# Hybrid retention and sparse-attention layer: norm weights applied before the transposes, rounding read straight from PSUM, a score accumulator zeroed in advance

## The chip, the core and the metric

One NeuronCore of a Trainium2 chip runs the whole layer as one program. The metric is the device time of one execution in microseconds, lower is better. Engines go by the profile's names: PE (TensorE matmul), PEld (its weight load), DVE (VectorE), ACT (ScalarE), POOL (GpSimd), SP (SyncE, which here only issues DMAs).

## What is computed

```
z = rmsnorm(x, norm_g) @ w_in            # x: 512 prompt tokens and 8 sample tokens, 2048 wide
q_r,k_r,v_r,g_r, q_a,k_a,v_a,g_a, q_i,k_i,w_i = split(z)
# group A: retention with rotary phase on q_r,k_r,v_r
# group B: indexer  score = sum_h w_i[h] * relu(q_i[h] . k_i);  keep the best keys per query;
#          softmax attention over those keys (samples also over 4096 cached keys each)
x = x + concat(A, B) @ w_out ;  y = rmsnorm(x, final_norm_g)
```

Every product with a weight matrix is done in three matmuls on values split in two: `Hh` is the activation rounded to the fp32r type, `Hl` the rest, and `Wh`, `Wl` the same of the weights; the sum is Wh·Hh + Wh·Hl + Wl·Hh. The first columns that are computed are the index keys `k_i` (128 columns) and the index weights `w_i` (16 columns), since the selection of keys needs them first. They are called chunk 0; their split weights are the tiles `W0h` (which also holds the high and the low part of the 16 columns side by side) and `W0l`.

## The kernel before

Each engine has its own instruction list, written out by hand; the order within a list is the order in the source, and engines meet at semaphores only.

The opening stage makes `Hh` and `Hl`. The 520 tokens are five tiles that arrive in the order 0, 1, 4, 2, 3 (tile 4 is the 8 samples; `ARRIVAL`). For every tile ACT sums the squares (`squares`), DVE makes the reciprocal root in a chain of 12 tiny operations (`norms`, first for tiles 0 and 1, then for the other three together) and multiplies the tile by it (`scale`). PE turns the tile, 2048 columns in 16 transposes, four to a PSUM bank, in banks 4 to 7 in rotation (`turn_tokens`, L1469). DVE multiplies each bank by the norm weights and writes it to SBUF (`gains`, L1017, into the idle tile `mix`), ACT rounds that to `Hh` (`high`, L577), and POOL subtracts the two to make `Hl` (L850), except for the last tile, where DVE does it (L1051). A bank may be filled again once `gains` has read it.

Meanwhile ACT rounds the chunk 0 weights (`hi`, L479) and DVE makes their low parts (`first_weights_low`, L1028 and L1030). PE then multiplies: index keys for tokens 0 to 255 (`index_keys(a, 0)` for the two halves a of the contraction), index weights, index keys for tokens 256 to 519 (`index_keys(a, 1)`), index weights again, and goes on with chunk 1 (`chunk(1, 0)`, L1451 to L1453). From there PE runs through chunks 1 to 8 (the index queries). Their low parts are made by POOL (L836), which takes the chunks in order once it has finished with the tokens.

After chunk 8 comes the scoring of the prompt: 48 rounds (16 heads times 3 blocks of queries) in which PE multiplies, ACT takes the relu and DVE adds it with its weight to the accumulator `bm`. The first head of a block writes `bm` (L1090), the other 15 add to it (L1088):

```
if h:
    v_.scalar_tensor_tensor(r, relu, wn, r, ALU.mult, ALU.add)
else:
    v_.tensor_scalar(r, relu, wn, None, ALU.mult)
```

ACT may not go on to the cached keys before all 48 are added. The rest of the program (cached keys, the selection, the other chunks, the output) is not touched.

Of the kernel before, what the change touches and what calls it, by code (L numbers as in the profile page):

```python
# [37 lines left out]
P = 128  # L38
DM = 2048
# [37 lines left out]
def build(nc, x_prompt, x_sample, cache_k, cache_v, cache_kidx, state_ret, page_table, norm_g, w_in,  # L77
# [3 lines left out]
    with ctx:  # L81
# [12 lines left out]
        mix = sb("mix", [P, KT, NT])  # L94
        ident = sb("ident", [P, P])
# [41 lines left out]
        W0h, _ = place("W0h", [P, KT, P + 2 * NIH], F32R, at["XT"][0])  # L137
        W0l, _ = place("W0l", [P, KT, P], F32R, at["junk"][0])
# [77 lines left out]
        def raw_tile(v, r):  # L216

            v = v % 16
            return mix[:, :, :].rearrange("p k t -> p (k t)")[:, 512 * v:512 * v + 512].rearrange("p (k t) -> p k t", k=4)[:, :, 0:r]

        bank = [ctx.enter_context(nc.psum_tensor(f"bank{i}", [P, 512], F32)) for i in range(8)]

# [3 lines left out]
        x_sq = sem("x_sq"); st4_set = sem("st4_set"); g_tr = sem("g_tr"); x_norm = sem("x_norm"); x_tr = sem("x_tr"); x_g = sem("x_g")  # L226
        h_hi = sem("h_hi"); h_lo = sem("h_lo"); h_lo_last = sem("h_lo_last")
# [107 lines left out]
        def _(sp):  # L335
# [29 lines left out]
            sp.wait_ge(x_in[1], 16)  # L365
# [99 lines left out]
        def _(act):  # L465
# [7 lines left out]
            def hi(n, a, step=None):  # L473
# [106 lines left out]
            for i in ARRIVAL:  # L580
# [250 lines left out]
        def _(pool):  # L831
# [13 lines left out]
            for pos in range(4):  # L845
                i = ARRIVAL[pos]
                for g in range(4):
                    v = 4 * pos + g
                    pool.wait_ge(h_hi, v + 1)
                    nc.gpsimd.tensor_tensor(Hl[:, 4 * g:4 * g + 4, tok(i)], raw_tile(v, rows(i)),  # L850
                                            Hh[:, 4 * g:4 * g + 4, tok(i)].bitcast(F32), ALU.subtract).then_inc(h_lo, 1)
# [114 lines left out]
        def _(dve):  # L966
# [42 lines left out]
            def gains(pos):  # L1009

                r = rows(ARRIVAL[pos])
                for g in range(4):
                    v = 4 * pos + g
                    dve.wait_ge(x_tr, v + 1)
                    if v >= 16:
                        dve.wait_ge(h_lo, v - 15)
                    v_.tensor_tensor(raw_tile(v, r),  # L1017
                                     bank[4 + v % 4][:, :].rearrange("p (k t) -> p k t", k=4)[:, :, 0:r],
                                     gin[:, 4 * g:4 * g + 4].unsqueeze(2).to_broadcast([P, 4, r]), ALU.mult).then_inc(x_g, 1)
# [906 lines left out]
```

## Time and profile before

| | us |
|---|---|
| median of 3 runs | 1240.18 (1239.47 to 1242.28) |
| the profiled execution | 1243.3, of which the span is 1241.5 |
| PE busy over the span | 1170.8 (94%) |
| DVE, ACT, POOL busy | 637.2, 452.3, 577.5 |

The span is the stretch that the trace covers; 1.8 us of the execution lie around it. Three views are used below: the timeline (instructions of one engine in order of time, with the idle time ahead of them), the table by windows (busy time of each engine and the clock granted to PE as a share of 2.4 GHz, in stretches between given times), and the table by groups of instructions. Times in rows count from the start of the span.

### The profile page before, as it was taken

To read this page: it belongs to the slowest core of one execution; us is meant where nothing else is said; L and a number is where in the kernel's file an instruction comes from. 1 tells how busy PE (TensorE), PEld (TensorE's weight loads), DVE (VectorE), ACT (ScalarE), POOL (GpSimd) and SP (SyncE) were. 2 spreads that over 40 slices of the span, in tenths; PEclk is the share of its full clock that TensorE was granted. 3 is DMA by queue.
4 is the path that set the end of the run, shared out by engine and by line. 5 is a ranking of instruction groups with operands and counts; after the bars stand their busy time and mean duration, and the time that the engine had idled before them with its cause. 6 is when DMAs were issued, how large, how long until landed. Compare 5 with 4: busy or idle time off the path is not lost.

```text
span 1241.5 us, 21876 instructions
## 1 busy us (share of the span) xinstructions
PE 1170.8 (94%) x9132; PEld 1109.9 (89%) x9132; DVE 637.2 (51%) x1201; ACT 452.3 (36%) x790; POOL 577.5 (47%) x267
## 2 busy tenths in 40 slices
PE   2899998988999999999999998999999998999995
PEld 2799997544999999999999998999999998999995
DVE  6700003898896997599998405254434537000013
ACT  5322323766223333333424232543434253323332
POOL 3525456042224222332536386848556474445450
PEclk9899998999999999999999999999999999999998
DMA  5423435185142321323343414454453424532313
GB/s 205 136 77 101 135 105 164 69 271 171 35 136 71 101 69 39 101 69 82 84 111 86 128 45 121 130 145 112 129 148 107 120 92 154 173 102 68 101 34 138
DMA packets 152838, 138.57 MB, mean 112 GB/s; under 512 B 4652, under 2 KB 145052, under 8 KB 151068
## 3 DMA queue, kind: packets, MB, share of 16 engines
q1 hardware_dynamic: 144500, 110.71, 29.9%
q0 software_dynamic: 6976, 22.03, 5.5%
q10 hardware_dynamic: 1280, 4.66, 1.0%
q8 instruction: 61, 1.00, 0.3%
q14 instruction: 21, 0.17, 0.0%
HBM read 127.01 MB, written 10.34 MB: 111 GB/s over the span
## 4 chain that ended last, share of the span: by engine, by line
PE 82%; DVE 10%; DMA 4%; issue 2%; ACT 1%; POOL 0%; DVEq 0%; ACTq 0%
PE bank L1451 24%; PE bank L1452 23%; PE bank L1453 23%; PE bank L1469 4%; DMA kx<-in_cache_kidx,pidx 3%; DVE bm L1088 2%; PE bank L1641 1%; PE bank L1659 1%; DVE cand L1154 1%; DVE top L1150 1%; DVE besti L1152 1%; DVE Hl L1051 1%; DMA XT<-in_x_prompt 1%; PE bank L1681 1%; DVE mix L1017 0%
## 5 line engine op out<-in xcount | busy, mean ns | idle before, releaser
L1451 PE MATMUL bank<-Hh,Wh 128*128 128x264 f32 (+2 forms) x2432 | 712.0, 293 | 2.1 <-DVE Hl L1288 0.8
L1452 PE MATMUL bank<-Hl,Wh 128*128 128x264 f32 (+2 forms) x2432 | 703.7, 289 | 0.6 <-issue 0.6
L1453 PE MATMUL bank<-Hh,Wl 128*128 128x264 f32 (+2 forms) x2432 | 702.4, 289 | 1.7 <-issue 1.6
L836 POOL TENSOR_TENSOR Wl<-Wraw,Wh 128x2048 fp32r<-128x2048 f32 x84 | 387.8, 4617 | 472.6 <-ACT Wh L484 472.2
L1451 PEld LDWEIGHTS bank<-Hh,Wh 128*128 128x128 f32 x2432 | 459.7, 189 | 6.7 <-issue 4.2
L1452 PEld LDWEIGHTS bank<-Hl,Wh 128*128 128x128 f32 x2432 | 459.7, 189 | 3.6 <-issue 3.3
L1453 PEld LDWEIGHTS bank<-Hh,Wl 128*128 128x128 f32 x2432 | 458.8, 189 | 2.8 <-issue 2.7
L484 ACT ACTIVATE Wh<-Wraw 128x2048 fp32r<-128x2048 f32 x84 | 160.4, 1911 | 365.9 <-PE bank L1453 365.7
L1391 DVE TENSOR_TENSOR Y<-Y,bank 128x512 f32 (+1 forms) x16 | 10.4, 685 | 159.2 <-PE bank L1469 159.2
L1072 DVE COPY QS<-mix 128x128 f32<-128x128 f32 x1 | 0.3, 281 | 146.1 <-ACT mix L490 146.1
L861 POOL DMA_INDIRECT kx<-in_cache_kidx,pidx x32 | 30.6, 955 | 55.8 <-PE bank L1469 48.8
L1469 PEld LDWEIGHTS bank<-ident,kx 128*128 128x128 f32 x256 | 27.3, 141 | 25.0 <-DMA kx<-in_cache_kidx,pidx 12.3
L1469 PE MATMUL bank<-ident,kx 128*128 128x128 f32 x256 | 34.5, 279 | 8.5 <-DMA kx<-in_cache_kidx,pidx 5.1
L1118 DVE MAX8 best<-scores 32x8 f32<-32x1025 f32 x32 | 38.9, 1217 | 6.7 <-ACT scores L673 5.7
L646 ACT ACTIVATE kT<-bank 128x512 f32<-128x512 f32 x64 | 35.0, 609 | 19.7 <-PE bank L1469 9.9
L891 POOL TENSOR_TENSOR XS<-XS,rot 128x520 f32<-128x520 f32 x16 | 21.1, 1321 | 44.5 <-ACT XW L542 44.5
L1150 DVE MAX8 top<-cand 8x8 f32<-8x1024 f32 x32 | 38.9, 1215 | 1.0
L1549 PE MATMUL bank<-kiT,mix 128*128 128x256 f32 (+2 forms) x96 | 34.6, 524 | 4.6 <-ACT relu L629 3.8
L1120 DVE FIND_INDEX8 besti<-best,scores 32x8 uint32<-32x1025 f32 x32 | 38.6, 1207 | 0.0
L1152 DVE FIND_INDEX8 besti<-top,cand 8x8 uint32<-8x1024 f32 x32 | 38.6, 1205 | 0.0
L1154 DVE MATCH_REPLACE8 cand<-top,cand 8x1024 f32<-8x1024 f32 x32 | 38.3, 1197 | 0.0
L1122 DVE MATCH_REPLACE8 scores<-best,scores 32x1025 f32<-32x1025 f32 x31 | 37.2, 1200 | 0.0
(251 smaller groups left out, 1243.6 us busy)
## 6 DMA issues: line engine op xcount, KB each, us to landing
Wraw<-in_w_in SPq DMA_DIRECT2D x36, 1024.0 KB
Wraw<-in_w_in SPq DMA_DIRECT2D x64, 512.0 KB
Wraw<-in_w_out SPq DMA_DIRECT2D x16, 1024.0 KB
XT<-in_x_prompt ACTq DMA_DIRECT2D x4, 1024.0 KB, 8.7
sp__99<-in_state_ret SPq DMA_DIRECT2D x8, 512.0 KB, 4.2
out<-sp__99 SPq DMA_DIRECT2D x8, 512.0 KB, 5.0
Y<-in_x_prompt SPq DMA_DIRECT2D x1, 4096.0 KB
out<-Y SPq DMA_DIRECT2D x4, 1024.0 KB
```

Source lines behind the costliest of these rows:

```text
L484: nc.scalar.activation(Wh[:, a, :, :], Wraw[:, a, :, :], ACT.Copy).then_inc(w_hi, 1)
L836: nc.gpsimd.tensor_tensor(Wl[:, a, :, :], Wraw[:, a, :, :], Wh[:, a, :, :].bitcast(F32), ALU.subtract).then_inc(w_lo, 1)
L1118: link(v_.max(top, row))
L1120: link(v_.max_index(besti[:, 8 * (k // 3):8 * (k // 3) + 8], top, row))
L1122: link(v_.match_replace(row, top, row, TAKEN))
L1150: link(v_.max(top, cand[:, :]))
L1152: link(v_.max_index(besti[0:NS, 8 * (k // 3):8 * (k // 3) + 8], top, cand[:, :]))
L1154: link(v_.match_replace(cand[:, :], top, cand[:, :], TAKEN))
L1451: mm(bank[i][:, 0:w], wh, Hh[:, kk, s], start=(a == 0 and k == 0), stop=False)
L1452: mm(bank[i][:, 0:w], wh, Hl[:, kk, s], start=False, stop=False)
L1453: last = mm(bank[i][:, 0:w], wl, Hh[:, kk, s], start=False, stop=(a == 1 and k == KC - 1))
L1469: return nc.tensor.transpose(out, in_, ident[0:k, 0:k])
```

## The change

1. The norm weights are no longer multiplied in after the transposes. A new DMA spreads `norm_g` over all partitions into a 128x2048 tile `gb`; it is the third load of ACT's queue. `scale` becomes one scalar_tensor_tensor that multiplies a tile by its reciprocal root and by `gb`. `gains` and the copy in `mix` are gone.
2. ACT rounds to `Hh` straight from the PSUM bank, and DVE makes all of `Hl`, reading the same bank (`low`). A bank may be filled again only when `low` has read it.
3. POOL makes the low parts of the chunk 0 weights in place of DVE. The tiles `W0h` and `W0l` lie in `mix` now, so ACT's rounding of them no longer waits for the transposes.
4. SP starts the weight loads when tile 2 has landed, not tile 1.
5. PE's list is in another order, and the index keys of tokens 256 to 519 are computed as tokens 256 to 383 and then 384 to 519.
6. `bm` is zeroed once (`memset`) when all tokens are done, and all 16 heads of a block use scalar_tensor_tensor.

```diff
@@ SP
-            sp.wait_ge(x_in[1], 16)
+            sp.wait_ge(x_in[2], 16)
@@ ACT, hi
                 if n == 0:
-                    act.wait_ge(x_tr, 8)
@@ ACT, high
-                    act.wait_ge(x_g, v + 1)
-                    nc.scalar.activation(Hh[:, 4 * g:4 * g + 4, tok(i)], raw_tile(v, rows(i)),
+                    act.wait_ge(x_tr, v + 1)
+                    nc.scalar.activation(Hh[:, 4 * g:4 * g + 4, tok(i)], turned_tile(v, rows(i)),
@@ ACT, loads of the tiles
+                if pos == 1:
+                    act.dma_start(gb[:, :], norm_g[0].partition_broadcast(P)).then_inc(g_row, 16)
@@ POOL
-            for pos in range(4):
...
-                    nc.gpsimd.tensor_tensor(Hl[:, 4 * g:4 * g + 4, tok(i)], raw_tile(v, rows(i)),
-                                            Hh[:, 4 * g:4 * g + 4, tok(i)].bitcast(F32), ALU.subtract).then_inc(h_lo, 1)
+            for a in range(2):
+                pool.wait_ge(w_hi, a + 1)
+                k = slice(KC * a, KC * a + KC)
+                nc.gpsimd.tensor_tensor(W0l[:, k, :], Wraw[:, a, :, 0:P], W0h[:, k, 0:P].bitcast(F32), ALU.subtract)
+                nc.gpsimd.tensor_tensor(W0h[:, k, P + NIH:P + 2 * NIH], Wraw[:, a, :, P:P + NIH],
+                                        W0h[:, k, P:P + NIH].bitcast(F32), ALU.subtract).then_inc(w_lo, 1)
+            pool.wait_ge(x_norm, 5)
             lo_loop(1, 10)
@@ DVE
-                v_.tensor_scalar(XT[0:r, i, :], XT[0:r, i, :], st4[0:r, column(i):column(i) + 1], None,
-                                 ALU.mult).then_inc(x_norm, 1)
+                v_.scalar_tensor_tensor(XT[0:r, i, :], XT[0:r, i, :], st4[0:r, column(i):column(i) + 1], gb[0:r, :],
+                                        ALU.mult, ALU.mult).then_inc(x_norm, 1)
+            def low(pos):
+                i = ARRIVAL[pos]
                 for g in range(4):
                     v = 4 * pos + g
+                    dve.wait_ge(h_hi, v + 1)
+                    v_.tensor_tensor(Hl[:, 4 * g:4 * g + 4, tok(i)], turned_tile(v, rows(i)),
+                                     Hh[:, 4 * g:4 * g + 4, tok(i)].bitcast(F32), ALU.subtract).then_inc(h_lo, 1)
...
+            link(v_.memset(bm[:, :], 0.0))
@@ DVE, scoring
-                        v_.scalar_tensor_tensor(r, relu[:, i % 2, 0:w], wn[:, t, h:h + 1], r, ALU.mult, ALU.add).then_inc(si_acc, 1)
-                    else:
-                        v_.tensor_scalar(r, relu[:, i % 2, 0:w], wn[:, t, h:h + 1], None, ALU.mult).then_inc(si_acc, 1)
+                    v_.scalar_tensor_tensor(r, relu[:, i % 2, 0:w], wn[:, t, h:h + 1], r, ALU.mult, ALU.add).then_inc(si_acc, 1)
@@ PE, turn_tokens
-                        pe.wait_ge(x_g, v - 3)
+                        pe.wait_ge(h_lo, v - 3)
@@ PE, chunk 0
-            pe.wait_ge(w_lo, 1)
             pe.wait_ge(h_lo, 8)
-            index_keys(0, 0)
+            pe.wait_ge(w_lo, 1)
+            index_keys(0, slice(0, CUT))
+            pe.wait_ge(w_lo, 2)
+            index_keys(1, slice(0, CUT)).then_inc(acc_done, 1)
             turn_tokens(2)
+            index_weights(slice(P, CUT))
             turn_tokens(3)
             turn_tokens(4)
-            pe.wait_ge(w_lo, 2)
-            index_keys(1, 0).then_inc(acc_done, 1)
-            index_weights(slice(P, CUT))
             pe.wait_ge(h_lo, 16)
-            pe.wait_ge(h_lo_last, 4)
-            index_keys(0, 1)
-            index_keys(1, 1).then_inc(acc_done, 1)
+            for a in range(2):
+                index_keys(a, slice(CUT, CUT + P))
+            pe.wait_ge(h_lo, 20)
+            for a in range(2):
+                last = index_keys(a, slice(CUT + P, NT))
+            last.then_inc(acc_done, 1)
             index_weights(slice(CUT, NT)).then_inc(acc_done, 2)
```

The order of two lists shows the move. DVE, before, from the end of the second `norms` to the page table's product (`XT` is a token tile, `W0l` and `W0h` the chunk 0 weights, `ptm` the page table's product):

```order
L986 SCALAR_TENSOR_TENSOR st<-rsq 128x3 [waits dve_chain]
L1028 TENSOR_TENSOR W0h<-Wraw,W0h 128x8x16 [waits w_hi,dve_chain]
L1030 TENSOR_TENSOR W0l<-Wraw,W0h 128x1024
L1006 TENSOR_SCALAR XT<-XT,st 8x2048
L1006 TENSOR_SCALAR XT<-XT,st 128x2048
...
L1017 TENSOR_TENSOR mix<-bank,gains_T 128x4x8 [waits x_tr] x4
...
L1017 TENSOR_TENSOR mix<-bank,gains_T 128x512 [waits h_lo,x_tr] x4
L1051 TENSOR_TENSOR Hl<-mix,Hh 128x4x128 [waits h_hi] x4
L1059 TENSOR_TENSOR ptm<-ptb,cols 128x256 [waits h_lo,h_lo_last,s_ptab,s_const]
```

The same stretch of DVE after the change:

```order
L989 SCALAR_TENSOR_TENSOR st<-rsq 128x3 [waits dve_chain]
L1018 TENSOR_TENSOR Hl<-bank,Hh 128x4x128 [waits h_hi,dve_chain]
L1018 TENSOR_TENSOR Hl<-bank,Hh 128x4x128 [waits h_hi] x7
L1009 SCALAR_TENSOR_TENSOR XT<-XT,st,gb 8x2048
L1009 SCALAR_TENSOR_TENSOR XT<-XT,st,gb 128x2048 x2
L1018 TENSOR_TENSOR Hl<-bank,Hh 128x4x8 [waits h_hi] x4
L1018 TENSOR_TENSOR Hl<-bank,Hh 128x4x128 [waits h_hi] x8
L1043 MEMSET bm 128x1280 [waits h_lo,s_ptab,s_const]
L1044 TENSOR_TENSOR ptm<-ptb,cols 128x256 [waits dve_chain]
```

The weights' low parts have left this list, the last three `scale` stand behind the `low` of tiles 0 and 1, and every `Hl` is here. PE, before, where the second half of the index keys begins (all rows of this stretch are index keys of 264 tokens; 48 of them):

```order
L1495 MATMUL bank<-Hh,W0h 128x264 [waits h_lo_last,h_lo]
L1496 MATMUL bank<-Hl,W0h 128x264
L1497 MATMUL bank<-Hh,W0l 128x264
```

After the change PE has 48 rows of the first kind below, and then 48 of the second:

```order
L1480 MATMUL bank<-Hh,W0h 128x128 [waits h_lo]
L1481 MATMUL bank<-Hl,W0h 128x128
...
L1480 MATMUL bank<-Hh,W0h 128x136 [waits h_lo]
L1481 MATMUL bank<-Hl,W0h 128x136
```

48 matmuls of 264 columns have become 96 of 128 or 136, each with its own load of 128 columns of weights.

## Rows read from the trace of the kernel before

**Rows 1.** PE by windows: busy, granted clock, DMA share, GB/s.
```profile
25.70:30.40 4.70, 0.00 (x0) 0.50 0.00 0
30.40:35.80 5.40, 5.36 (x24) 0.50 0.68 204
...
51.50:56.20 4.70, 4.70 (x21) 0.50 0.71 223
56.20:63.40 7.20, 7.20 (x61) 0.99 0.48 148
```
**Rows 2.** Timeline of PE: start, duration, line, out<-in, idle before and its releaser.
```profile
45.80 0.22 PE L1504 MATMUL bank<-Hh,W0h 128*32 128x128 f32 x1
45.86 0.22 PE L1505 MATMUL bank<-Hl,W0h 128*32 128x128 f32 x1
...
51.49 0.56 PE L1495 MATMUL bank<-Hh,W0h 128*128 128x264 f32 x1 [5.17 <-DVE Hl L1051]
...
63.45 0.34 PE L1451 MATMUL bank<-Hh,Wh 128*128 128x392 f32 x1
```
**Rows 3.** Timeline of DVE and POOL, 13 to 31 us.
```profile
13.34 2.48 DVE L1006 TENSOR_SCALAR XT<-XT,st 128x2048 f32<-128x2048 f32 x2
...
17.84 9.89 POOL L850 TENSOR_TENSOR Hl<-mix,Hh 128x512 fp32r<-128x512 f32 x8 [17.38 <-ACT Hh L577]
...
18.40 3.22 DVE L1017 TENSOR_TENSOR mix<-bank,gains_T 128x512 f32<-128x512 f32 x5 [0.16 <-PE bank L1469]
...
26.56 1.19 DVE L986 SCALAR_TENSOR_TENSOR rsq<-rsq 128x3 f32<-128x3 f32 x1
27.78 0.16 DVE L984 TENSOR_TENSOR rsq<-rsq 128x3 f32<-128x3 f32 x1
```
**Rows 4.** Timeline of DVE and POOL, 45 to 52 us.
```profile
45.75 5.59 DVE L1051 TENSOR_TENSOR Hl<-mix,Hh 128x512 fp32r<-128x512 f32 x2
...
45.78 5.02 POOL L836 TENSOR_TENSOR Wl<-Wraw,Wh 128x2048 fp32r<-128x2048 f32 x1 [0.50 <-ACT Wh L484]
```
**Rows 5.** Timeline of ACT, 8 to 24 us, and the four tile loads from issue to landing.
```profile
8.94 1.91 ACT L568 ACTIVATE junk<-XT 128x2048 f32<-128x2048 f32 x1 [1.06 <-DMA XT<-in_x_prompt]
...
17.15 1.75 ACT L577 ACTIVATE Hh<-mix 128x512 fp32r<-128x512 f32 x3
...
23.66 1.15 ACT L479 ACTIVATE W0h<-Wraw 128x1152 fp32r<-128x1152 f32 x1
...
DMA to landing us min/median/max: 5.1/8.7/11.9
```
**Rows 6.** Group: the last scalar_tensor_tensor of the program, 2048 elements.
```profile
L1428 DVE SCALAR_TENSOR_TENSOR Ys<-Ys,st,gfb x1: 2332/2332/2332, 1233.7 to 1233.7; 8x2048 f32<-8x2048 f32 x1
```
**Rows 7.** Groups of weight loads, 0 to 64 us: busy, mean ns.
```profile
L1505 PEld LDWEIGHTS bank<-Hl,W0h 128*32 128x32 f32 x32 | 3.5, 108 | 0.2
...
L1452 PEld LDWEIGHTS bank<-Hl,Wh 128*128 128x128 f32 x2 | 0.4, 188 | 0.0
```
**Rows 8.** Pieces of the chain that ended last: start, us, what.
```profile
14.69 4.43 PE bank L1469 x20
...
35.93 1.10 PE bank L1469 x16
...
421.49 2.23 PE bank L1659 x20
```
**Rows 9.** Timeline of DVE and POOL in the scoring.
```profile
206.12 4.42 DVE L1090 TENSOR_SCALAR bm<-relu,wn 128x256 f32<-128x256 f32 x1 [1.61 <-ACT relu L629]
210.65 5.21 DVE L1088 SCALAR_TENSOR_TENSOR bm<-relu,wn,bm 128x256 f32<-128x256 f32 x9
...
219.91 0.42 DVE L1090 TENSOR_SCALAR bm<-relu,wn 128x384 f32<-128x384 f32 x1
220.50 10.72 DVE L1088 SCALAR_TENSOR_TENSOR bm<-relu,wn,bm 128x384 f32<-128x384 f32 x15 [0.17 <-ACT relu L629]
...
205.89 4.50 POOL L836 TENSOR_TENSOR Wl<-Wraw,Wh 128x2048 fp32r<-128x2048 f32 x1 [4.43 <-ACT Wh L484]
```

More of the change, by code:

```diff
@@ L1033, in _ @@
+            link(v_.tensor_copy(gains_T[:, :], bank[3][:, 0:KT + NH]))
             norms(0, 2)
+            dve.wait_ge(g_row, 16)
             scale(0)
             scale(1)
-            dve.wait_ge(g_tr, 1)
-            link(v_.tensor_copy(gains_T[:, :], bank[3][:, 0:KT + NH]))
-            gains(0)
-            gains(1)
             norms(2, 5)
-            first_weights_low(0)
+            low(0)
+            low(1)
             scale(QT)
             scale(2)
-            first_weights_low(1)
@@ L1045, in _ @@
-            gains(2)
             scale(3)
-            gains(3)
-            gains(4)
-            for g in range(4):
-                dve.wait_ge(h_hi, 17 + g)
-                v_.tensor_tensor(Hl[:, 4 * g:4 * g + 4, tok(3)], raw_tile(g, P),
-                                 Hh[:, 4 * g:4 * g + 4, tok(3)].bitcast(F32), ALU.subtract).then_inc(h_lo_last, 1)
+            low(2)
+            low(3)
+            low(4)
             dve.wait_ge(s_const, 80)
             dve.wait_ge(s_ptab, 16)
-            dve.wait_ge(h_lo, 16)
@@ L1489, in _, with index_keys @@
             turn_tokens(1)
-            def index_keys(a, half):
-                s, out = part_tokens(half), bank[half][:, 0:part_width(half)]
+            def index_keys(a, s):
+                half = s.start >= CUT
+                out = bank[half][:, s.start - CUT * half:s.stop - CUT * half]
                 for k in range(KC * a, KC * a + KC):
-                    mm(out, W0h[:, k, 0:P], Hh[:, k, s], start=(k == 0), stop=False)
-                    mm(out, W0h[:, k, 0:P], Hl[:, k, s], start=False, stop=False)
+                    wh = W0h[:, k, 0:P]
+                    mm(out, wh, Hh[:, k, s], start=(k == 0), stop=False)
+                    mm(out, wh, Hl[:, k, s], start=False, stop=False)
                     last = mm(out, W0l[:, k, :], Hh[:, k, s], start=False, stop=(k == KT - 1))
@@ L1503, in index_weights @@
                 for k in range(KT):
-                    mm(out, W0h[:, k, P:P + 2 * NIH], Hh[:, k, s], start=(k == 0), stop=False)
-                    last = mm(out, W0h[:, k, P:P + 2 * NIH], Hl[:, k, s], start=False, stop=(k == KT - 1))
+                    wi = W0h[:, k, P:P + 2 * NIH]
+                    mm(out, wi, Hh[:, k, s], start=(k == 0), stop=False)
+                    last = mm(out, wi, Hl[:, k, s], start=False, stop=(k == KT - 1))
                 return last
+            pe.wait_ge(h_lo, 8)
             pe.wait_ge(w_lo, 1)
-            pe.wait_ge(h_lo, 8)
-            index_keys(0, 0)
+            index_keys(0, slice(0, CUT))
+            pe.wait_ge(w_lo, 2)
+            index_keys(1, slice(0, CUT)).then_inc(acc_done, 1)
             turn_tokens(2)
+            index_weights(slice(P, CUT))
             turn_tokens(3)
             turn_tokens(4)
-            pe.wait_ge(w_lo, 2)
-            index_keys(1, 0).then_inc(acc_done, 1)
-            index_weights(slice(P, CUT))
             pe.wait_ge(h_lo, 16)
-            pe.wait_ge(h_lo_last, 4)
-            index_keys(0, 1)
-            index_keys(1, 1).then_inc(acc_done, 1)
+            for a in range(2):
[4 more added lines that the diff above has]
+            last.then_inc(acc_done, 1)
             index_weights(slice(CUT, NT)).then_inc(acc_done, 2)
```

39 lines of the change are left out of this document (11 added, 28 removed).

## Prediction

> **What bounds the kernel now.** The page first: PE is busy 94% of the span, so the question is where PE stands still or runs slowly. The windows of PE show two stretches of the opening at half clock: nothing from 25.7 to 30.4 us, then 24 matmuls at a granted 0.50 (1.2 GHz) until 35.8; and 21 matmuls at 0.50 from 51.5 to 56.2, before the clock is back at 2.4 GHz [rows 1]. The timeline says who is waited for: at 51.49 PE had stood 5.17 us for DVE's last `Hl` [rows 2]. Chunk 1, from which PE runs without a gap to the scoring, starts at 63.45 [rows 2]. Everything later hangs on that instant: PE's list goes on in fixed steps, and POOL, ACT and SP follow PE. So the opening's gain is 63.45 minus the new start of chunk 1.
>
> Why the opening is slow can be read on DVE and POOL. While POOL made `Hl` (8 in 9.89 us, 1.24 us each), DVE's three-element operations took 1.19 us; the first after POOL's last took 0.16 [rows 3]. Later two subtractions of DVE took 5.59 us beside one of POOL's of 5.02 [rows 4]: an operation that reads two tensors from SBUF stands until POOL's running one has ended, and the two take turns. A DVE operation that reads its large operand from PSUM does not stand: five of L1017 took 3.22 us, 0.64 each, with POOL at work beside them [rows 3].
>
> The second place is the scoring. The first L1090 took 4.42 us, exactly POOL's L836 beside it (205.89 to 210.39), and it is on the chain: ACT and PE wait for it [rows 9].
>
> **The opening, step by step.** All times from here on are estimates from the rows.
>
> Loads. The first 1 MB tile landed at 5.9 us, the second at 8.9, the last at about 14.6 (the loads are issued from 0.8 to 2.7, and took 5.1 to 11.9) [rows 5]. The two between 8.9 and 14.6 are 2.8 us each, so `gb`, 1 MB more, lands at about 12 and everything after it 2.6 us later: tile 2 at 14.5, tile 3 at 17.2. `gb` costs DVE nothing, since `norms` ends at 13.34. But ACT's squares, back to back until 17.15 [rows 5], now end at 19.2: **2 us later**, and `Hh` begins only then. The chunk 0 weights (requested at 14.5) land by about 21, when ACT wants them.
>
> `scale` costs 2.3 us in place of 1.24 [rows 6, 3]: tile 0 is ready at 15.6, tile 1 at 17.8. PE's 16 transposes of a tile take 3.6 us at the low clock (20 in 4.43) [rows 8]; `norms` for the other tiles runs from 19.2 to 21.6, in 0.2 us steps since POOL is idle. ACT rounds tile 0 from 19.2, 0.58 each [rows 5]. `low` of tile 0: 21.7 to 24.2, four of 0.64. The banks go back to PE one by one, tile 1 is turned by 26.0, ACT's last `Hh` of it is at 26.6, and `low` ends at **27.4**. ACT rounds the first weights 21.6 to 22.8 and the second 26.7 to 27.9 (1.15 each) [rows 5]. POOL's low part of the first half is ready at 25.6 (1024 elements at half of L836's 4.5 us, 2.3, and 0.4 for the 16 columns) [rows 9]. PE begins the index keys at 27.5, not 30.4.
>
> Now the new wait. DVE starts the `scale` of the samples at 27.4; POOL's second low part comes at 27.9 and, both reading two SBUF operands, they take turns as in [rows 4]: DVE to 29.7, POOL to 32.0, DVE (tile 2) to 34.2, POOL's 16 columns to **34.6**. PE, which finished the first half of the contraction by 32.6 at the low clock, stands until then. With the clock granted high, 24 matmuls take 2.8 us (37.5), the samples' transposes 1.1 (16 in 1.10) [rows 8], the index weights 2.0 (32 at 0.06) [rows 2]: 40.6. Behind POOL's wait stand only chunk 1's low parts, which need ACT much later.
>
> Tiles 2 and 3 then go round PE, ACT and DVE; DVE at 0.64 is the slowest of the three. PE has made its last transpose about 4.5 us on: 45.1; the last `Hl` is there at about 47, while PE is at tile 2's keys.
>
> The split. 48 matmuls of 264 columns (0.12 each at the high clock) become 96 of 128 or 136. What one costs is not in the trace. From below 0.060: a 32-column load with 128 moving columns [rows 2]. From above 0.188: a load of 128 columns, if nothing hides it [rows 7]. The nearest row has 128 columns on both sides, though in plain f32: 20 of L1659 in 2.23 us, 0.112 each [rows 8]. I take 0.112, because the load of 128 columns is 80 ns longer than that of 32 [rows 7], that is 0.84 ns a column or 107 ns for 128. So 96 x 0.112 = 10.8 where 48 x 0.12 = 5.8 was: 5 us of the gain goes here. The Trainium skill (TensorE: Matmul & The Clock Gate, LDWEIGHTS) gives columns / 1.2 ns for a load, 107 ns too, but in "Back-to-back issue gap" a sustained 81 ns for N=128; by that figure the sum would be 3.0 us better. No run here shows it for fp32r.
>
> 45.1 + 10.8 + 3.9 (32 index weights at 0.12) = **59.8**. POOL has chunk 1's first low part at about 52.5, so it is not late. The opening gains 63.45 - 59.8 = 3.65 us.
>
> **The scoring.** Head 0 as a scalar_tensor_tensor still reads two SBUF tensors (relu and bm), as L986 did, which stood for 1.19 us [rows 3]. POOL starts at 205.89 and DVE at 206.12 [rows 9], and both shift alike. So the stall of 4.2 us stays, and an operation of 0.5 us stands in place of one of 0.15: +0.3. For the other two blocks the step grows from 0.59 (219.91 to 220.50) to 10.72/15 = 0.72 [rows 9], and as much for 512 columns: +0.26. Together **+0.55 us**. The Trainium skill (SBUF — State Buffer, Who interferes with whom) says that a DVE instruction with two SBUF inputs contends with a GpSimd one that reads SBUF, and a tensor_scalar in its two-port mode does too; so by it no form of head 0 escapes. The trace agrees in L986. The memset of `bm` (1280 columns, about 1.3 us) lies at 47 us, beside PE's keys; uncovered it would be 1.3.
>
> Sum: -3.65 + 0.55 = -3.1. Against the profiled 1243.3 us that is 1240.2. The profiled execution is 3.1 above the median of the runs; against the median it is **1237.1**. From this central sum about 1.5 us either way is the uncertainty of landings and turns.
>
> **Rivals.**
>
> A, the clock is low when it matters. PE's work from 15.6 us on comes in pieces of 3 to 5 us with gaps of 1.3 to 3. Twice the clock fell or stayed low in gaps like the one before 51.5, and it rose 5.4 and 4.7 us after a restart [rows 1]. If it is low from 34.6, 24 keys take 5.2 in place of 2.8, and transposes of the samples add some 0.1: -3.1 + 2.4 = -0.7, or 1239.5. Chance 0.27.
>
> B, the weight loads hide. At 0.060 the split costs 5.8 us: 5.0 less, -8.1, or 1232.1. For it: loads hide well elsewhere, 188 ns loads under matmuls 0.12 apart. Against: those have 256 columns to hide under. Chance 0.10.
>
> C, head 0 no longer stands behind POOL: the 4.2 us stall goes, -7.3, or 1232.9. Against it speaks L986. Chance 0.08.
>
> D, slower. The load of 128 columns is not hidden at all by 128 moving ones: 0.188 each, 96 x 0.076 = 7.3 more, +4.2, or 1244.4. It decides from 0.17 us a matmul upwards (0.112 + 5.6/96), where the sum is 2.5 us on the other side. For it: a turn of 128 columns takes about as long as its load. Against: L1659. Chance 0.08.
>
> E, that the change does nothing because POOL takes over the port: this would need `norms` to be held as now. POOL's list has nothing to run before 22.8, so no. Chance 0.03, 1240.
>
> **From cases to numbers.** A measurement of this kernel tells about 0.2%, 2.5 us. The forecast has 0.44, of which two thirds (0.30) lie beyond 2.5 us. Faster: 0.30 + 0.10 + 0.08 = 0.48. Same: the rest of the forecast 0.14, A 0.27 and E: 0.43. Slower: 0.09. The range runs from B and C at 1232.5 to A's upper edge, 1240.8 (the low clock kept for the transposes and the index weights too, +1.3). The forecast's own range is 1235.6 to 1238.6.
>
> **What would show it.** Squares ending at 19 and not 17 us. `norms` for three tiles in about 2.4 us. PE waiting near 33 us for POOL's W0h. Matmuls of 128 columns 0.11 us apart. Chunk 1 at 59 to 61. Head 0 of the scoring still 4 to 5 us. I am wrong in the mechanism if chunk 1 starts before 57 or after 63, if POOL's second low part is not held behind `scale`, or if head 0 takes under 1 us.

## The result, and the profile after

The changed kernel takes 1243.18 us (median of 20 runs, 1240.97 to 1245.63), the kernel before in the same session 1240.95 (20 runs, 1239.41 to 1242.9): ratio 1.0016, 95% interval 1.0009 to 1.0023. That is 2.2 us more, not 3.1 less. A second measurement, further down, gave 1.0013 (1.0004 to 1.0022). The profiled execution of the changed kernel took 1243.84 us, its span is 1241.9.

The beginning went as forecast. The timeline of ScalarE (start, duration, line, out<-in, idle before and its releaser) shows the last square ending at 19.1, two us later than in [rows 5], and the timeline of VectorE the norms in steps of 0.2 us, the low parts of tiles 0 and 1 and then the three scales:

```profile
17.20 1.91 ACT L569 ACTIVATE junk<-XT 128x2048 f32<-128x2048 f32 x1 [0.56 <-DMA XT<-in_x_prompt]
...
19.11 2.04 ACT L578 ACTIVATE Hh<-bank 128x512 fp32r<-128x512 f32 x4
```

```profile
21.42 0.16 DVE L989 SCALAR_TENSOR_TENSOR st<-rsq 128x3 f32<-128x3 f32 x1
21.62 3.28 DVE L1018 TENSOR_TENSOR Hl<-bank,Hh 128x512 fp32r<-128x512 f32 x5
...
27.38 6.85 DVE L1009 SCALAR_TENSOR_TENSOR XT<-XT,st,gb 8x2048 f32<-8x2048 f32 x3
```

The last row is where it went wrong. Three scales in 6.85 us are 2.28 each with nothing between them: VectorE and POOL did not take turns. POOL's timeline shows the same from the other side. The first low part takes 2.37 us, the second, of the same size, 8.57; it started at 27.87 and ended at 36.4, 2.2 us behind the last scale:

```profile
22.28 2.37 POOL L851 TENSOR_TENSOR W0l<-Wraw,W0h 128x1024 fp32r<-128x1024 f32 x1 [21.82 <-ACT W0h L480]
24.60 0.45 POOL L852 TENSOR_TENSOR W0h<-Wraw,W0h 128x128 fp32r<-128x128 f32 x1
27.87 8.57 POOL L851 TENSOR_TENSOR W0l<-Wraw,W0h 128x1024 fp32r<-128x1024 f32 x1 [2.81 <-ACT W0h L480]
36.40 0.44 POOL L852 TENSOR_TENSOR W0h<-Wraw,W0h 128x128 fp32r<-128x128 f32 x1
```

TensorE's windows (busy, granted clock, DMA share, GB/s) and its timeline show the price. TensorE stood (had nothing to run) from 32.3 to 36.9, the granted clock fell from 2.4 to 1.2 GHz in the stand, and the keys of the second weight half came at 0.213 us apart until 41.3, not at 0.119:

```profile
31.00:33.00 2.00, 1.30 (x10) 1.00 0.00 0
33.00:35.00 2.00, 0.00 (x0) 0.93 0.00 0
35.00:37.00 2.00, 0.10 (x1) 0.50 0.00 0
37.00:39.00 2.00, 2.00 (x10) 0.50 0.43 91
39.00:41.00 2.00, 2.00 (x11) 0.50 1.07 379
```

```profile
36.90 0.58 PE L1480 MATMUL bank<-Hh,W0h 128*128 128x256 f32 x1 [4.60 <-POOL W0h L852]
...
41.99 1.15 PE L1452 MATMUL bank<-ident,XT 8*128 8x8 f32 x16
...
49.24 0.31 PE L1480 MATMUL bank<-Hh,W0h 128*128 128x128 f32 x1
...
60.00 0.28 PE L1490 MATMUL bank<-Hh,W0h 128*32 128x264 f32 x1
...
63.85 0.34 PE L1434 MATMUL bank<-Hh,Wh 128*128 128x392 f32 x1
```

The 96 short matmuls from 49.24 to 60.00 are 0.112 us each, as forecast. Chunk 1 starts at 63.85 (before, profiled: 63.45 [rows 2]; forecast: 59.8).

In the scoring, POOL's subtraction (206.28 to 210.78) holds head 0 again. The group of VectorE's operations has a maximum of 4548 ns beside a median of 618:

```profile
L1073 DVE SCALAR_TENSOR_TENSOR bm<-relu,wn,bm x48: 483/618/4548, 206.5 to 244.4; 128x256 f32<-128x256 f32 x16, 128x384 f32<-128x384 f32 x16, 128x512 f32<-128x512 f32 x16
```

"Chunk 1" below is the start of the first `Hh,Wh` matmul in the profile of the kernel in question; "scoring" is the time from the first `kiT,mix` matmul to the first transpose of cached keys `kx`. From chunk 1 to the scoring it is 140.7 us in every profile here, so what chunk 1 gains or loses arrives there whole. For the changed kernel these are 204.56 to 244.23, 39.67 us.

### The profile page after: what moved, and what is told of

It reads as the page before. It is cut to its first block, busy times and chain, and to the rows that moved or that the text cites. A ratio compares the mean times of both kernels' runs of the same rounds, so it can differ in the third digit from the quotient of the medians.

```text
span 1241.9 us, 21947 instructions
## 1 busy us (share of the span) xinstructions
PE 1172.9 (94%) x9180; PEld 1111.9 (90%) x9180; DVE 630.2 (51%) x1194; ACT 452.3 (36%) x790; POOL 571.1 (46%) x255
## 4 chain that ended last, share of the span: by engine, by line
PE 81%; DVE 9%; DMA 3%; POOL 2%; issue 2%; ACT 2%; another core or an unknown queue 0%; ACTq 0%; DVEq 0%; POOLq 0%
PE bank L1434 23%; PE bank L1435 23%; PE bank L1436 23%; PE bank L1452 5%; DVE bm L1073 3%; DMA kx<-in_cache_kidx,pidx 2%; PE bank L1630 1%; PE bank L1648 1%; DMA XT<-in_x_prompt 1%; DVE cand L1137 1%; DVE top L1133 1%; DVE besti L1135 1%; PE bank L1566 1%; PE bank L1670 1%; POOL rowf L888 1%
## 5 line engine op out<-in xcount | busy, mean ns | idle before, releaser
L1452 PEld LDWEIGHTS bank<-ident,kx 128*128 128x128 f32 x256 | 27.3, 141 | 27.5 <-DMA kx<-in_cache_kidx,pidx 12.9
L1452 PE MATMUL bank<-ident,kx 128*128 128x128 f32 x256 | 34.3, 279 | 11.3 <-DMA kx<-in_cache_kidx,pidx 6.0
L1538 PE MATMUL bank<-kiT,mix 128*128 128x256 f32 (+2 forms) x96 | 34.1, 516 | 4.7 <-ACT relu L632 3.9
```

The source lines that it names most:

```text
L1452: return nc.tensor.transpose(out, in_, ident[0:k, 0:k])
```

## The experiments

### Who is let into SBUF, and when

**POOL first (e1).** In the changed kernel:
```
+            dve.wait_ge(w_lo, 2)
             scale(QT)
             scale(2)
             scale(3)
```


> Changed kernel with one wait more: VectorE waits for POOL's second low part (w_lo 2) ahead of the last three scales. If it is the three scales, one behind the other with no wait between them, that keep POOL out for 6.85 us, POOL's subtraction of 128x1024 then takes about 2.4 us as the first one did, w_lo 2 is there at about 30.7 us instead of 36.9, TensorE goes from the keys of the first half of the weights straight on at 32.3, and at a clock that is granted high or low the scales end 3 us later than in the changed kernel (about 37.5 instead of 34.2). The keys of the second weight half then end at about 37 (low clock) or 35 (high), and the new turns of tiles 2 and 3 wait for their scales: chunk 1 starts 1.5 to 4 us earlier than 63.86, total 1239 to 1241.5. Rival, the wait for POOL is nothing but a late TensorE start and everything is made up later: chunk 1 at 63.9, total as the changed kernel, 1243.2. Rival with the other sign: the scales moved back by 3 us now end last, and tiles 2, 3 and the sample rows are later: chunk 1 at 65 to 66, total 1245.

1236.91 us, ratio to before 0.9946 (0.9933 to 0.9959). POOL and VectorE:
```profile
27.72 2.38 POOL L851 TENSOR_TENSOR W0l<-Wraw,W0h 128x1024 fp32r<-128x1024 f32 x1 [2.80 <-ACT W0h L480]
30.05 0.46 POOL L852 TENSOR_TENSOR W0h<-Wraw,W0h 128x128 fp32r<-128x128 f32 x1
```
```profile
30.55 6.86 DVE L1009 SCALAR_TENSOR_TENSOR XT<-XT,st,gb 8x2048 f32<-8x2048 f32 x3 [3.23 <-POOL W0h L852]
```
8.57 us have become 2.38. TensorE runs from 27.36 to the last index weight without a stand, the second key half goes at 0.119 throughout, and chunk 1 is at 56.57: 7.3 us earlier, though three scales end 3.2 us later. I had expected 1.5 to 4, because I took those scales for the next thing to be waited for. They weren't: tile 2's turns started at 37.74, right behind TensorE's own index weights. A stand of 4.6 us was worth 7.3: 2.3 of the rest are the keys behind it, which took 2.8 us at the high clock in place of 5.1 at the low. The next experiment, whose opening is that of the changed kernel, took 1243.17 us beside it, 6.3 more.

**A wait that is already fulfilled (e2).**
```
             scale(QT)
+            dve.wait_ge(x_sq, 5)
             scale(2)
+            dve.wait_ge(x_sq, 5)
             scale(3)
```


> Changed kernel with a wait that is long fulfilled (x_sq 5, reached at 19.2 us) ahead of the second and the third of the last three scales; nothing else moves. Theory: it is the missing wait that lets VectorE's instructions follow each other with POOL shut out; with a wait between them POOL gets its turn after the first scale, as it did before between VectorE's gain multiplications: w_lo 2 at about 33 to 35 us, the last scale ends 2 to 3 us later. Rival: a fulfilled wait costs no gap, and POOL is let in only where VectorE really stands; then the scales stay one block of 6.85 us and w_lo 2 stays at 36.9, total 1243.2 as the changed kernel.

1243.17 us, ratio 1.0 (0.9991 to 1.001). The scales remain one block and POOL's operation takes 8.57 us:
```profile
27.34 6.86 DVE L1009 SCALAR_TENSOR_TENSOR XT<-XT,st,gb 8x2048 f32<-8x2048 f32 x3
```
The first theory, that any wait between the scales lets POOL in, fell.

**A real gap (e5).** The same two lines with `x_norm, 3` and `x_norm, 4`, which the scale ahead raises itself when it is done.

> Changed kernel in which the second and the third of the last three scales wait for the completion of the scale ahead of them (x_norm 3, x_norm 4), so that VectorE really stands for some tens of ns between them. A wait that is fulfilled already let nobody in (e2_satisfied_wait: 6.86 us in one block, POOL's operation 8.57). Theory: POOL gets the port when VectorE has nothing running, however short that is, as it did between the chained operations of the norms in the kernel before. Then POOL's 128x1024 subtraction ends after the first scale, at about 32, its 16 columns after the second one at 34.5, the last scale ends at 36.5 to 37.5, and TensorE's second key half starts at 34.6, not at 36.9; chunk 1 up to 2.3 us earlier than 63.86, or 4 more if the clock stays high. Rival: some tens of ns are too short, VectorE's next operation comes first again: w_lo 2 at 36.9, total as the changed kernel.

1240.89 us, ratio 0.9985 (0.9976 to 0.9994). VectorE and POOL:
```profile
27.10 9.18 DVE L1009 SCALAR_TENSOR_TENSOR XT<-XT,st,gb 8x2048 f32<-8x2048 f32 x3
```
```profile
27.59 4.09 POOL L851 TENSOR_TENSOR W0l<-Wraw,W0h 128x1024 fp32r<-128x1024 f32 x1 [2.79 <-ACT W0h L480]
31.63 2.50 POOL L852 TENSOR_TENSOR W0h<-Wraw,W0h 128x128 fp32r<-128x128 f32 x1
```
Three scales and POOL's 2.3 us between them make 9.18, and POOL's two operations wait for one scale each: the turn-taking that the prediction counted on, with the second low part at 34.1 (forecast 34.6). Chunk 1 is at 60.52. So these scales alternate with POOL when each has to wait for the result of the one ahead, and shut it out when the next one is ready. The norms' operations in [rows 3] are of the first kind: each waits for the one ahead. Those of [rows 4] aren't, and they show that this is no general rule. ScalarE and VectorE in the kernel before:
```profile
39.08 4.82 ACT L577 ACTIVATE Hh<-mix 128x512 fp32r<-128x512 f32 x8 [1.56 <-DVE mix L1017]
```
```profile
L1051 DVE TENSOR_TENSOR Hl<-mix,Hh x4: 678/1381/4989, 43.1 to 46.4; 128x512 fp32r<-128x512 f32 x4
```
ScalarE had written the last `Hh` at 43.90, so the last two subtractions, at 45.75 and 46.35, were ready one behind the other. POOL's operation started at 45.78, it took 5.02 us where it took 4.50 in [rows 9], and the last subtraction took 4.99 in place of 0.68: POOL was let in between two ready operations. The changed kernel has such a stretch as well: from 1014 to 1023 us VectorE's subtractions and POOL's, each of 512 columns, went by turns (1.78 us a subtraction on VectorE, 1.73 on POOL). Three ready scales (scalar_tensor_tensor, 2048 elements) keep POOL out and ready subtractions (tensor_tensor, 512 elements) don't. Whether the kind of operation, its length or something else decides is open; no run here separates them.

**VectorE makes the second low part (e8).** POOL's pair of subtractions for the second half moved to VectorE, ahead of the scales; TensorE waits for them. POOL has a memset of one column left there.

> Changed kernel in which VectorE, not POOL, makes the second low part of the first weights (128x1024 and 16 columns), right ahead of the last three scales; POOL has nothing there. The subtraction reads SBUF twice and should take 1.1 us plus 0.2: low part ready at about 29.4 (e1_pool_first: 30.5), scales end at 36.3 (37.4), clock granted high from 30.7. Chunk 1 at 55.4, that is 1.1 us ahead of e1_pool_first and 8.4 ahead of the changed kernel: total 1235.8. Rival, if the stand of VectorE isn't what set the rest: same as e1_pool_first, 1236.9. If it is 1243, the port wasn't the cause.

1238.19 us, ratio 0.9953 (0.9935 to 0.9971). The low part is ready at 29.2 and chunk 1 starts at 56.74, not at 55.4. Once nobody is shut out, the low part is early in either version (TensorE gets to it at about 32), and chunk 1 doesn't depend on who makes it (56.57 and 56.74).

### What TensorE's stand costs

**Work in the stand (e9).** Ahead of the wait for the second low part TensorE transposes the identity matrix 38 times into a bank that nobody reads:
```
+            for _ in range(38):
+                turn(bank[3][:, 0:P], ident[:, :])
             pe.wait_ge(w_lo, 2)
```


> Changed kernel in which TensorE, while it waits for POOL's second low part, transposes the identity 38 times into a bank that nobody reads (38 x 0.112 = 4.3 us, from 32.3 to 36.6). Theory of the clock: the pitch falls to 0.213 in the second key half because TensorE stood for 4.6 us; if it works through the wait the pitch stays 0.119, and the 24 keys take 2.9 us in place of 4.6 to 5.1: chunk 1 at 61.7 to 62.3 in place of 63.86, total 1.6 to 2.1 us under the changed kernel. Rival: the fill ends too late, or the clock falls all the same: chunk 1 at 63.9 or later.

1240.54 us, ratio 0.9997 (0.9987 to 1.0007); chunk 1 at 62.82. It didn't test what it was meant to: in this profile the first key half ran at the high rate from 27.05, so the fill ended at 34.3 and TensorE stood for 2.1 us more. The clock fell after even that:
```profile
30.00:34.30 4.30, 4.30 (x40) 1.00 0.01 4
34.30:36.40 2.10, 0.02 (x1) 0.99 0.00 0
36.40:38.00 1.60, 1.56 (x7) 0.50 0.26 35
```

**The same with 56 transposes (e16).**

> e9_fill_the_wait with 56 transposes of the identity in place of 38, 6.3 us. In e9 the first key half ran at the high rate from 27.05 (24 keys in 3 us), the fill ended at 34.3, and TensorE stood for 2.1 us: the clock fell to 0.50 all the same. If the fill now covers the stand (30.0 to 36.3), the second half stays at 0.119 a matmul: 36.5 to 39.4, chunk 1 at 61.3 to 61.7. If the first half is at the low rate, as in the changed kernel (until 32.3), the fill ends at 38.6, the keys at 41.5 and chunk 1 is at 63.4. Rival: the clock falls whatever TensorE does there: keys 4.5 to 5.1 us, chunk 1 at 62.8 to 65.

1240.63 us, ratio 0.999 (0.9981 to 0.9999). No stand, no fall:
```profile
30.00:33.00 3.00, 3.00 (x28) 1.00 0.00 0
33.00:36.00 3.00, 3.00 (x30) 1.00 0.03 5
36.00:38.00 2.00, 2.00 (x21) 1.00 0.14 23
38.00:40.00 2.00, 2.00 (x20) 1.00 0.99 329
```
The fill ends late (the second half starts at 37.40, not 36.9), and yet its 24 matmuls are done at 40.4 in place of 42.0, and chunk 1 is at 62.29, 1.6 earlier. The clock's part of the stand is thus 2.1 us, the 0.5 of the late fill added.

### The split of the index keys

**Unsplit, with POOL first (e6).** The keys of tokens 256 to 519 in one piece, 48 matmuls of 264 columns behind the last low part.
```
-            pe.wait_ge(h_lo, 16)
-            for a in range(2):
-                index_keys(a, slice(CUT, CUT + P))
             pe.wait_ge(h_lo, 20)
             for a in range(2):
-                last = index_keys(a, slice(CUT + P, NT))
+                last = index_keys(a, slice(CUT, NT))
```


> e1_pool_first with the index keys of tokens 256 to 519 in one piece again: 48 matmuls of 264 columns after the last low part (h_lo 20, at about 44.0) in place of 96 of 128 and 136 from 41.96. By the pitches measured (0.112 and 0.120) 96 take 10.7 us and 48 take 5.8: TensorE starts them 2 us later and ends 2.9 us earlier, chunk 1 at 53.7 in place of 56.57, total 1234.0 if all of it arrives at the end. Rival: TensorE's stand of 2 to 4 us ahead of the unsplit keys lets the clock fall, they take 10 us at half clock, and chunk 1 is at 56 to 58: no gain, or a loss of 1 us.

1234.73 us, ratio 0.9933 (0.9918 to 0.9948), chunk 1 at 55.37: 1.2 earlier than with the split, not 2.9. The rival came in half. TensorE stood for 1.73 us ahead of them and the clock fell:
```profile
42.00:44.00 2.00, 0.29 (x3) 1.00 0.00 0
44.00:47.00 3.00, 2.98 (x14) 0.55 0.01 3
47.00:50.00 3.00, 3.00 (x24) 0.88 0.00 0
```

**Unsplit alone (e15)**, in the changed kernel as it is.

> The changed kernel with the split of the index keys of tokens 256 to 519 undone and nothing else. The split lets TensorE begin at 49.3 and costs 96 x 0.112 = 10.7 us; without it the 48 matmuls begin at about 51.4 behind the last low part. With the clock high: 51.4 + 5.8 + 3.9 = 61.1, 2.8 us ahead of 63.86. Rival, as in e6_unsplit: TensorE's stand of 2 us ahead of it brings the clock down for part of the keys, and 0.8 to 1.4 us of it remain: chunk 1 at 62.5 to 63.1.

1240.02 us, ratio 0.9991 (0.9982 to 1.0); chunk 1 at 62.60, 1.25 earlier, again behind a stand of 1.73 us with the clock at 0.73 and 0.50. The split costs 4.9 us of TensorE time, saves the stand and the low clock, and loses 1.2 us on balance.

### The row's load

**No row load (e10)** (with POOL first): VectorE sets the row of norm weights to ones, so this output is that of weights of one.

> e1_pool_first without the 1 MB load of the norm weights' row: VectorE sets the row to ones at the start instead, so the output is that of norm weights of one. It measures what the load costs. From the landings: the squares end at 17.2 instead of 19.1, the first keys start 1.9 us earlier (25.5 instead of 27.4), chunk 1 at 54.6 in place of 56.57, total 1235.0. Rival: the clock rises when it rises (30.7), so that what comes earlier runs at half rate longer: of 1.9 us 0.9 or less remain at chunk 1. Second rival: norms of tiles 2 and 3 or the weights' load take its place, and the keys start at 27.4 as before.

1235.0 us, ratio 0.9952 (0.9937 to 0.9968). The squares end at 17.2 us, but the norms behind them start at 17.89 and not before, because the scales of tiles 0 and 1 end there (they begin at 13.36 and take 4.61 us):
```profile
13.36 4.61 DVE L1007 SCALAR_TENSOR_TENSOR XT<-XT,st,gb 128x2048 f32<-128x2048 f32 x2
17.89 0.16 DVE L998 TENSOR_SCALAR st<-st 128x3 f32<-128x3 f32 x1
```
The first keys start at 25.90 in place of 27.36, chunk 1 at 54.95 in place of 56.57. The load costs 1.6 us there, of the 2 that the squares lose.

### The scoring

**Undone in the changed kernel (e3), and done alone in the kernel before (e4)** (there the accumulator is zeroed behind `QS`, since its bytes are in use until about 62 us). The edit of `e3`:
```
-            link(v_.memset(bm[:, :], 0.0))
...
                     if h:
                         dve.wait_ge(si_acc, i)
-                    v_.scalar_tensor_tensor(r, relu[:, i % 2, 0:w], wn[:, t, h:h + 1], r, ALU.mult, ALU.add).then_inc(si_acc, 1)
+                        v_.scalar_tensor_tensor(r, relu[:, i % 2, 0:w], wn[:, t, h:h + 1], r, ALU.mult, ALU.add).then_inc(si_acc, 1)
+                    else:
+                        v_.tensor_scalar(r, relu[:, i % 2, 0:w], wn[:, t, h:h + 1], None, ALU.mult).then_inc(si_acc, 1)
```


> Changed kernel with its last part undone: head 0 of each tile is again written by a product with one number, without the accumulator as a third operand, and the accumulator is not zeroed ahead. The traces give the scoring stage 0.51 to 0.55 us more with the change. So here: scoring shorter by 0.5 us, total 1242.6 to 1242.8. Rival: the stage's difference is taken up by the wait for the cached keys behind it, and the total stays 1243.2; other rival: the early zeroing and the changed scoring also delay the cached keys, and it brings more, 1.5 us.

> Kernel of before with the last part of the change alone: accumulator zeroed early (behind the zeroing of the query rows, about 62 us), head 0 by the same operation as the other heads. Expected 0.5 us more than before, 1241.5. Rival: no difference, since scoring isn't last in its stage; other rival: 1.5 us or more, if the loss in the stage of the cached keys comes from here.

Undone: 1243.75 us, ratio 1.0009 (1.0 to 1.0017). Alone: 1243.14, ratio 0.9997 (0.9987 to 1.0008). Neither total can tell 0.5 us. The scoring in the traces can: with the old form 39.56, 39.33 and 39.04 us (before, before again, undone), with the new one 39.67 to 39.93 in twelve profiles. By their means, 39.31 and 39.75, the new form costs 0.4 us, near the forecast 0.55.

**ReLU in PSUM (e7)** (with POOL first). ScalarE writes the ReLU into the bank that it reads, VectorE reads it there, and TensorE takes a bank again once VectorE is through. ScalarE's own wait for VectorE goes:
```
-                    if i >= 2:
-                        act.wait_ge(si_acc, i - 1)
-                    nc.scalar.activation(relu[:, i % 2, 0:w], bank[4 + i % 4][:, 0:w], ACT.Relu).then_inc(si_relu, 1)
+                    nc.scalar.activation(bank[4 + i % 4][:, 0:w], bank[4 + i % 4][:, 0:w], ACT.Relu).then_inc(si_relu, 1)
...
-                        pe.wait_ge(si_relu, i - 3)
+                        pe.wait_ge(si_acc, i - 3)
```


> e1_pool_first in which the scoring's ReLU is written in place, into the PSUM bank that it reads, and VectorE multiplies and adds from there (one operand in SBUF, the accumulator, in place of two); TensorE takes a bank again when VectorE has read it. Theory: head 0 of the first tile stands 4.2 us because two of its operands lie in SBUF while POOL subtracts; with one operand in PSUM it takes 0.4 to 0.6 us and the stage is 4 us shorter, total about 1232.9. Rival: it is POOL's writing or the accumulator in SBUF alone that holds VectorE, the first operation still takes 4.5 us, and the total stays at 1236.9 or grows by 1 us for the later release of the banks. Second rival: the time comes back as a wait for the gathered cached keys, for which TensorE stood already in e1_pool_first.

1232.65 us, ratio 0.9915 (0.9898 to 0.9932). The group of VectorE's operations and POOL's subtraction beside them:
```profile
L1072 DVE SCALAR_TENSOR_TENSOR bm<-bank,wn,bm x48: 483/617/751, 199.7 to 233.1; 128x256 f32<-128x256 f32 x16, 128x384 f32<-128x384 f32 x16, 128x512 f32<-128x512 f32 x16
```
```profile
199.49 4.52 POOL L837 TENSOR_TENSOR Wl<-Wraw,Wh 128x2048 fp32r<-128x2048 f32 x1 [4.43 <-ACT Wh L485]
```
The maximum is 751 ns in place of 4548, with POOL at work from 199.49 to 204.01; the scoring takes 36.14 us (197.76 to 233.90). The stall of this operation hung on its second large input in SBUF, the ReLU's result, and not on the accumulator alone.

**The same alone (e14)**, in the changed kernel.

> The changed kernel with the ReLU in PSUM alone (the opening is left as it is). In e7_relu_in_psum the scoring came out 3.55 us shorter than in e1_pool_first and the total 4.3. If the two places are independent: chunk 1 at 63.85, scoring 3.6 us shorter than the changed kernel's 39.7, total 3.5 to 4.3 us under it (1238.2 to 1239). Rival: here the cached keys' gather, issued by POOL right behind the same subtraction, then ends last, and less than 2 us remain.

1239.39 us, ratio 0.9984 (0.9975 to 0.9993). Scoring 36.17 us (204.60 to 240.77), 3.5 less: the two places are independent. The ratio lies 2.9 to 3.2 thousandths under the two of the changed kernel, 3.6 to 4.0 us, with intervals of about 1.1 us either way: within these all of it arrives.

### All that helped, and the controls

**All together (e11)**: POOL first, ReLU in PSUM, unsplit keys with 18 transposes of the identity ahead.

> All that helped together: POOL's low part first (e1), ReLU in PSUM (e7), unsplit keys of tokens 256 to 519 (e6) with 18 transposes of the identity ahead of them, so that TensorE doesn't stand for its 2 us (e6 lost half of its gain to a clock of 0.50 from 44.2 to 48.5). Chunk 1 at 53.7 if the clock stays high (e6: 55.37, e1: 56.57), 2.9 us ahead of e7: total 1229.8 if all of it arrives. Rival: the cached keys' gather takes the gain, since in e6 the 1.2 us of chunk 1 were gone behind the first cached keys: then 1232.7 as e7.

1229.19 us, ratio 0.9909 (0.989 to 0.9929), the fastest kernel here; chunk 1 at 53.79, and the keys at the high clock throughout:
```profile
42.00:44.00 2.00, 2.00 (x22) 1.00 0.00 0
44.00:47.00 3.00, 3.00 (x27) 1.00 0.01 3
47.00:50.00 3.00, 3.00 (x27) 1.00 0.03 5
```
Against the unsplit kernel above, the 2 us of useless transposes bring 1.6 us at chunk 1. How much of it arrives at the end isn't shown. Against `e7` chunk 1 starts 3.3 us earlier, but the ratio is only 0.0006 lower, with intervals of 0.002 either way: the median is 3.5 us lower, and that of the kernel before, measured beside each, was 2.7 us lower beside `e11` too. The rival, that the cached keys' gather takes the gain, stands.

**The changed kernel again (e12).**

> The changed kernel once more, unaltered, for the spread of what lies behind the scoring. In its first profile the cached keys' stage took 76.3 us against 74.2 before and the stage ahead of 756 us took 2.2 us less. If these are chance, this profile shows other numbers for both, chunk 1 at 63.9 and 0.5 us more in the scoring again; against the kernel before 1.0 to 1.0016. If the cached keys' stage is again 76.3 it belongs to the change.

1242.55 us, ratio 1.0013 (1.0004 to 1.0022); chunk 1 at 63.81. From the first transpose of cached keys to the start of the last group of products with them it took 63.3 us (244.21 to 307.49), where the first profile of the same kernel took 65.05 (244.23 to 309.28). Over all eighteen profiles this stage, in which TensorE waits for gathered keys, lies between 62.1 and 65.1. The three with the opening of the kernel before have 62.5 to 63.0, with a mean of 62.7; the fifteen others have a mean of 63.5, and `e3`, with the changed opening, has the shortest. The scatter is larger than the difference of the means, so a cost of the change in this stage is neither shown nor excluded.

**The kernel before again (e13).**

> The kernel before, unaltered, as a control for the small differences and for its stage of cached keys. If what the changed kernel loses there is chance, this profile's stage lies within 73.4 to 76.3 us like the others, and the ratio is 1.000 within 0.001. If it belongs to the change, this one shows 74.2 or less, as the first profile of before (74.2) and e4_only_scoring (74.0) did.

1240.74 us, ratio 0.9995 (0.9986 to 1.0004). The stage of cached keys took 62.5 us (241.87 to 304.34), a little less than in the first profile of the kernel before (63.0). That is what the expectation gave for a cost of the change; the 62.1 of `e3` speaks against it. The clearer finding is in the opening. Its chunk 1 starts at 61.83, 1.6 us earlier than in the profile from which I predicted:
```profile
61.83 0.34 PE L1451 MATMUL bank<-Hh,Wh 128*128 128x392 f32 x1
```
Here are TensorE's windows of this profile; [rows 1] show 0.50 up to 35.8 and up to 56.2.
```profile
30.50:32.00 1.50, 1.41 (x6) 0.50 0.24 27
32.00:34.00 2.00, 2.00 (x13) 0.62 0.94 321
34.00:36.00 2.00, 2.00 (x25) 1.00 0.78 216
...
52.00:54.00 2.00, 2.00 (x11) 0.50 1.08 383
54.00:56.00 2.00, 2.00 (x18) 1.00 0.22 68
```
The same work started at the same time (30.59 and 30.44), and the clock came back some two us earlier, twice. The opening of the kernel before thus has no fixed end: 63.45, 61.83, and 63.02 in the kernel with only the scoring changed. The changed opening nearly has: 63.85, 63.81, 64.11, 63.72 and 63.90 in the five profiles that leave its course alone (the changed kernel twice, `e2`, `e3`, `e14`), with TensorE starting on the second keys at 36.67 to 36.90 in all of them, behind POOL.

## Why the prediction was wrong

**The loads, squares, norms, first low parts: right.** Squares to 19.1 (19.2), norms 19.24 to 21.6, POOL's first low part at 25.05 (25.6), first keys at 27.52 (27.5).

**"DVE and POOL take turns": the step that failed.** I had the second low part at 34.6; it came at 36.84, because VectorE's three scales follow each other without a gap and POOL isn't let in between. I had carried the turn-taking of two subtractions [rows 4] over to scales that nothing had shown beside POOL. With a gap put in, the forecast order appeared to within 0.5 us (`e5`), and with POOL put first 7.3 us came back (`e1`). Even with the order that I forecast, `e5` is only 1.9 us under the kernel before by its ratio, with chunk 1 at 60.52.

**"With the clock granted high": the second failure, and a consequence.** I had named the low clock as rival A with 0.27 and priced it at 2.4 us. It came true, and the runs put it at 2.1 (`e16`). It should have had a larger chance: the gap ahead of the second keys was forecast by my own numbers at 2 us (32.6 to 34.6), and the runs show falls behind stands of 2.1 us (`e9`) and 2.3 us (`e5`). In `e5`, where POOL's low part came at the time that I forecast, the keys took 4.5 us (34.19 to 38.66).

**From 42 us on: right in every length.** Samples' turns to the last turn 7.2 us (forecast 7.6), 96 keys at 0.112 (0.112), index weights 3.9 (3.9). From the second keys' start to chunk 1 it is 26.95 us where I had 25.2 (34.6 to 59.8). Chunk 1 at 63.85 against 59.8 is 2.3 for the shut-out, 2.3 for the clock over the keys (5.1 in place of 2.8), less 0.5 in the turns and keys behind. I said that the mechanism is wrong if chunk 1 starts after 63; it is, in this one step.

**"63.45 minus the new start": a start taken from one execution.** The opening gain was counted against a profile that was 3.1 us above the median. Another profile of the same kernel has 61.83 and took 1238.73 us. I took the 3.1 off the total and left 63.45 standing, which counted a late clock as something that the change would remove. Against the mean of the three unchanged openings, 62.77, the mean of the five changed ones, 63.88, is 1.1 us slower, and with the 0.4 of the scoring 1.5: inside the interval of the ratio, 1.1 to 2.9 us. Three starts that scatter by 1.6 us carry this only roughly. The rest, 0.7, isn't assigned to a place; it is as large as the difference of the means in the stage of cached keys (0.8), which scatters by more. The sign is itself near the noise: `e2`, with the changed opening and scoring, is at 1.0 (0.9991 to 1.001).

**The split: the size right, the balance untested.** 4.9 us more TensorE time, as forecast (5). What I didn't work out is that undoing it brings back only 1.2 us, since the unsplit keys begin behind a stand that lowers the clock.

**The scoring: right.** Head 0 still stands (4548 ns), the new form costs 0.4 (0.55). Rival C, that it stands no longer, fell. For this operation what matters is that both large inputs lie in SBUF. That is also what the Trainium skill says (SBUF — State Buffer, Who interferes with whom), and `e7` agrees with 751 ns in place of 4548. The number of inputs isn't all of it: the old form of head 0 has one large input in SBUF and stood as long, 4.42 us [rows 9]. Rivals B (loads hidden, 0.060) and D (0.188 a matmul) fell to the pitch of 0.112; so did the 81 ns of the Trainium skill (TensorE: Matmul & The Clock Gate, Back-to-back issue gap), by which the sum would have been 3.0 us better. Slower was right in sign for a reason that none of the rivals had.

## What to carry to other kernels

Before you move an operation next to another engine's that shares SBUF with it, don't take turns for granted because another pair of operations took them: here three ready scales shut POOL out until the last, the same scales let it in after each when each waited for the result of the one ahead, and shorter subtractions alternated with it though they were ready. Put the short operation that somebody waits for first; here one wait of VectorE turned +2 us into -6.7 against the kernel before. Price TensorE's stands with the low clock behind them, and where one can't be removed, work that is thrown away can pay for itself. Take a start time that you want to improve on from more than one execution, when the clock changes just ahead of it.

## What the runs showed of the hardware that I had not expected

- Three scales of VectorE (scalar_tensor_tensor, 2048 elements, two inputs in SBUF), ready one behind the other, held a POOL operation of 2.37 us for 8.57 us. A wait that was fulfilled long before didn't change it (8.57), a wait for the predecessor's result did (4.09). Ready subtractions of 512 elements let POOL in between (4.99 us in place of 0.68, [rows 4]).
- An operation with a single large input in SBUF can be held as well. The same tensor_scalar took 3.98 us in the changed kernel, beside POOL's low parts (52.00 to 61.28), and 0.24 in the kernel before, where POOL's had ended at 55.77:
```profile
57.35 3.98 DVE L1047 TENSOR_SCALAR pidx<-pidf,cols 128x32 uint32<-128x32 f32 x1
```
```profile
56.53 0.24 DVE L1062 TENSOR_SCALAR pidx<-pidf,cols 128x32 uint32<-128x32 f32 x1
```
- VectorE's subtractions with one operand in PSUM ran through POOL's two-operand one without slowing it: 3.28 us for five, beside 2.37.
- The table by windows gave a granted clock of 1.00 from 27 to 31 us in the changed kernel while 256-column keys came at 0.213 us apart, as they do at 37 to 41 us where the column says 0.50. In that stretch of the trace the pitch has to be read, not the column.
- In the opening TensorE's clock fell behind stands of 1.73 us (`e6`, `e15`), 2.1 us (`e9`) and 2.3 us (`e5`). It stayed at 2.4 GHz in `e1`, where no such stand was, and in `e11` and `e16`, where useless transposes filled it. The length of the stand alone doesn't settle it: among the cached keys it stayed at 1.00 through one of 1.75 us (`e11`, to 238.50) and one of 1.79 us (`e15`, to 254.05).
- Mean granted clock and time go together from run to run of the kernel before: of the 33 beside `e13` those at 0.981 and 0.982 took 1242.29 to 1243.65 us, those at 0.984 1239.42 to 1241.83.
